# The experts' stage of a hybrid encoder block: pipelined blocks and a scatter that adds

## What is computed

```python
gsel = top-1 of 4 groups                      # per token
eid  = gsel * 8 + top-2 of the 8 experts of that group
gate = p_group * top_p / sum(top_p)
# rows sorted by expert, each expert's rows cut into blocks
y_e  = (silu(xb @ w_gate[e]) * (xb @ w_up[e])) @ w_down[e]
h    = h + sum over the token's two experts of gate * y_e
```

## Time and profile before

| what | value |
|---|---|
| median of 3 runs | 3429.85 us (3428.99 to 3430.35) |
| span of the profiled execution | 3433.8 us |
| PE busy | 3059.8 us, 89% of the span |
| DVE, ACT, POOL busy | 45%, 32%, 10% |
| first gate instruction of `experts` | 2463.71 us |
| last group of down instructions begins | 3424.35 us |

### The profile page before, as it was taken

The page is one execution under the profiler, slowest core; times in us unless marked ns, Lnnn a source line. Parts: engine busy times, 40 slices in busy tenths (PEclk is TensorE's granted clock), DMA queues, the critical chain, the costliest instruction groups (busy, mean ns, idle before and its releaser), DMA issues. The chain is left out here.

```text
span 3433.8 us, 82115 instructions
## 1 busy us (share of the span) xinstructions
PE 3059.8 (89%) x33176; PEld 2305.5 (67%) x33177; DVE 1553.3 (45%) x3540; ACT 1115.5 (32%) x2626; POOL 352.2 (10%) x478
## 2 busy tenths in 40 slices
PE   5999999999968888879999959995399999999999
PEld 4777777777845555578888845553277777777776
DVE  3675666656657777623333337774011111111111
ACT  2343334333447777722222213432011111111111
POOL 0000000000000000000000000000422222222222
PEclk9999999999979999989999989997699999999999
DMA  5211121112130110011111144324577777767663
GB/s 209 65 59 56 52 66 57 57 49 70 57 100 7 48 47 9 9 60 42 42 42 42 41 178 147 135 98 149 75 282 280 283 279 276 283 231 262 218 243 112
DMA packets 211799, 413.98 MB, mean 121 GB/s; under 512 B 29738, under 2 KB 95530, under 8 KB 210016
## 3 DMA queue, kind: packets, MB, share of 16 engines
q1 hardware_dynamic: 191184, 360.07, 30.1%
q0 software_dynamic: 20368, 50.44, 4.2%
HBM read 334.97 MB, written 88.31 MB: 123 GB/s over the span
## 5 line engine op out<-in xcount | busy, mean ns | idle before, releaser
L287 PE MATMUL pj_big<-pj_xnT,pj_w_in 128*128 128x256 f32 x2816 | 646.1, 386 | 10.2 <-issue 8.8
L287 PEld LDWEIGHTS pj_big<-pj_xnT,pj_w_in 128*128 128x128 f32 x2816 | 545.8, 194 | 95.3 <-issue 16.3
L1753 PEld LDWEIGHTS ex_pg<-ex_wg,ex_xT 128*64 128x64 f32 x5120 | 292.1, 137 | 63.9 <-issue 61.2
L1753 PE MATMUL ex_pg<-ex_wg,ex_xT 128*64 128x128 f32 x5120 | 319.7, 275 | 6.8 <-issue 5.4
L1753 PE MATMUL ex_pu<-ex_wu,ex_xT 128*64 128x128 f32 x5120 | 312.9, 273 | 0.0
L1762 PE MATMUL ex_py<-ex_wd,ex_hT 128*64 128x512 f32 x1280 | 310.0, 603 | 1.7
L1753 PEld LDWEIGHTS ex_pu<-ex_wu,ex_xT 128*64 128x64 f32 x5120 | 291.3, 137 | 0.0
L1833 DVE TENSOR_TENSOR ex_hh<-ex_sg,ex_pu 128x128 f32<-128x128 f32 x160 | 46.0, 287 | 484.7 <-PE ex_pu L1753 484.7
L1202 PE MATMUL mg_po<-mg_w_out,mg_mix 128*128 128x512 f32 x512 | 230.2, 609 | 5.6 <-DVE mg_mix L1434 3.9
L708 ACT ACTIVATE at_e<-at_sc,at_nmx 128x512 f32<-128x512 f32 (+3 forms) x320 | 196.4, 620 | 115.2 <-DVE at_nmx L747 115.0
L1805 ACT ACTIVATE ex_sg<-ex_pg 128x128 f32<-128x128 f32 x160 | 44.3, 277 | 581.1 <-PE ex_pg L1753 581.1
(11 more groups left out here) (277 smaller groups left out, 4986.5 us busy)
## 6 DMA issues: line engine op xcount, KB each, us to landing
ex_wg<-in_w_exp_gate SPq DMA_DIRECT2D x32, 2048.0 KB
ex_wu<-in_w_exp_up SPq DMA_DIRECT2D x32, 2048.0 KB
ex_wd<-in_w_exp_down SPq DMA_DIRECT2D x32, 2048.0 KB
chunks_s<-pj_st SPq DMA_DIRECT2D x32, 642.0 KB, 4.0
rw_raw<-chunks_s SPq DMA_DIRECT2D x32, 642.0 KB, 3.9
pj_xt<-in_x SPq DMA_DIRECT2D x20, 512.0 KB, 3.7
qk_s<-pj_qo SPq DMA_DIRECT2D x64, 128.0 KB, 1.9
mg_xin<-in_x SPq DMA_DIRECT2D x8, 1024.0 KB, 6.1
```

The costliest lines, as they stand in the source:

```text
L287: ins = pe.matmul(out, lhs, rhs, start=(k == 0), stop=(k == KC - 1))
L1753: ins = pe.matmul(out[j * BT:(j + 1) * BT, 0:P], lhs, w[:, k, c0:c0 + P], start=(k == 0), stop=(k == KC - 1))
```

## The change

It touches the `experts` stage and, by NB and the rounding of the counts, the table in `dispatch`.

- Gate and up weights lie in one tile `wgu`, and the two products are computed together: one matmul streams 256 columns of gate and 256 of up into one bank `pgu` (`gate_up`, 32 instructions of 512 columns). Silu, the multiplication, the transposes of h and the copy to `hT` are done once for a block, over 256 columns for each partition.
- The blocks overlap on PE: `body(b)` transposes h of block b-1, transposes x of block b+1, computes gate and up of block b, and then the down product of block b-1. The first block's `gate_up` stands ahead of the loops, the last one's `down` behind them. The body that crosses to the next expert (`turn`) uses the new expert's `wgu` and the old one's `wd`. For that, every expert must have two blocks or more, so the count is rounded up to at least 2; NB grows from 96 to 128 and the table with it.
- `acc` is gone. DVE computes `yb` = gate * `py`, and the scatter has `compute_op=ALU.add`: the DMA adds the rows to `out`. x is gathered one block further ahead.
- SP waits for `s_pgu` in place of `s_pu`.

```diff
-NB = 2 * S // BT + NE
+NB = 2 * S // BT + 2 * NE
...
-            chain(dve.tensor_scalar(nb[:, :], nb[:, :], 1.0, None, ALU.add))
+            chain(dve.tensor_scalar(nb[:, :], nb[:, :], 1.0, 1.0, ALU.max, ALU.add))
...
-            for s0, b0, b1 in ((0, 0, 4), (1, 4, NB + 1)):
+            for s0, b0, b1 in ((0, 0, 4), (1, 4, NB + 2)):
...
                 n, first = blocks_of(sp, 4 * i + q - 2)
-                sp.wait_ge(s_pu, 2 * (first + n))
+                sp.wait_ge(s_pgu, first + n)
                 weights_in(sp, bass.ds(EPG * q + i, 1), q % 2)
                 sp.wait_ge(s_py, first + n)
                 weights_out(sp, bass.ds(EPG * q + i, 1), q % 2)
...
-            def rows_acc(x):
-                pool.indirect_dma_start(acc[x][:, :], None, out2, bass.IndirectOffsetOnAxis(idx[:, 0:1], 0),
-                                        bounds_check=LAST, oob_is_err=False).then_inc(s_acc[x], 16)
+            def next_x(b):
+                pool.wait_ge(s_x, 16 * b + 32)
+                pool.sem_inc(s_apart, 1)
+                pool.tensor_copy(idx[:, :], tab[:, bass.ds(b + 2, 1), 0]).then_inc(s_idx, 1)
+                pool.wait_ge(s_idx, b + 3)
+                pool.sem_inc(s_apart, 1)
+                pool.wait_ge(s_px, b + 2)
+                pool.sem_inc(s_apart, 1)
+                gather_x()
...
                 pool.indirect_dma_start(out2, bass.IndirectOffsetOnAxis(idy[:, 0:1], 0), yb[x][:, :], None,
-                                        bounds_check=LAST, oob_is_err=False).then_inc(o_y, 16)
+                                        bounds_check=LAST, oob_is_err=False, compute_op=ALU.add).then_inc(o_y, 16)
...
+            def gate_up(x):
                 for k in range(KC):
                     lhs = xT[:, k % 4, k // 4 * BT:(k // 4 + 1) * BT]
                     for j in range(2):
-                        c0 = 2 * P * j + P * part
-                        ins = pe.matmul(out[j * BT:(j + 1) * BT, 0:P], lhs, w[:, k, c0:c0 + P],
+                        ins = pe.matmul(pgu[j * BT:(j + 1) * BT, :, :], lhs, wgu[x][:, k, :, j * HE:(j + 1) * HE],
                                         start=(k == 0), stop=(k == KC - 1))
...
+            def body(b, x, before, i, y):
+
+                transpose_h(before)
                 pe.wait_ge(s_xT, b + 1)
                 pe.wait_ge(s_x, 16 * b + 32)
                 transpose_x()
+                gate_up(x)
+                down(before, i, y)
...
             pe.wait_ge(s_x, 16)
             transpose_x()
+            pe.wait_ge(s_xT, 1)
+            pe.wait_ge(s_x, 32)
+            transpose_x()
+            pe.wait_ge(s_wi[0], 32)
+            gate_up(0)
...
+            def gate(b, x):
+                dve.wait_ge(s_py, b + 1)
+                dve.wait_ge(o_y, 16 * b + 16)
+                dve.tensor_scalar(yb[x][:, :], py[:, :], tab[:, bass.ds(b, 1), 1], None, ALU.mult).then_inc(s_yb, 1)
...
-                    dve.scalar_tensor_tensor(yb[x][:, :], py[:, :], tab[:, bass.ds(b, 1), 1], acc[x][:, :],
-                                             ALU.mult, ALU.add).then_inc(s_yb, 1)
```

More of the change, by code:

```diff
@@ new lines, in transpose_h, with down @@
+            def transpose_h(b):
+                pe.wait_ge(s_hh, b + 1)
+                pe.wait_ge(s_hT, b + 1)
+                for part in range(2):
+                    ins = pe.transpose(phT[:, part * P:(part + 1) * P], hh[:, part * P:(part + 1) * P], ident[:, :])
+                ins.then_inc(s_phT, 1)
+            def down(b, i, x):
+                pe.wait_ge(s_wo[x], 16 * i + 16)
+                pe.wait_ge(s_yb, b + 1)
+                pe.wait_ge(s_hT, b + 2)
+                for part in range(2):
+                    for j in range(2):
+                        for n in range(2):
+                            ins = pe.matmul(py[n * BT:(n + 1) * BT, :], hT[:, part, j * BT:(j + 1) * BT],
+                                            wd[x][:, 2 * j + part, n * HD:(n + 1) * HD],
+                                            start=(part == 0 and j == 0), stop=(part == 1 and j == 1))
+                ins.then_inc(s_py, 1)
@@ L1784, in body, with rest, turn @@
[L1784 to L1785 removed]
+                gate_up(x)
+                down(before, i, y)
+            def rest(i, x, n, first):
+                with pe.Fori(0, n - 1) as j:
+                    body(below(first + j + 1, NB - 1), x, below(first + j, NB - 1), i, x)
+            def turn(i, x, n, first):
+                pe.wait_ge(s_wi[1 - x], 32 * (i + x) + 32)
+                pe.sem_inc(s_apart_pe, 1)
+                body(below(first + n, NB - 1), 1 - x, below(first + n - 1, NB - 1), i, x)
```

169 lines of the change are left out of this document (71 added, 98 removed).

## The result

The changed kernel takes **3380.94 us** (median of 4 runs, 3375.09 to 3383.68), against 3429.42 us (median of 4) before on the same chip: a ratio of 0.9856, 95% interval 0.9842 to 0.987. Forecast were 3404.2 us with a range of 3388 to 3429.

What follows compares the result with a forecast made beforehand. PE was taken as the bound: blocks falling from 12.02 to 11.53 us save 39.2 over 80, and 13.5 is added, so 3433.8 - 39.2 + 13.5 = 3408.1 of span; the median, 3.95 below, is 3404.2 us, range 3388 to 3429.

Steps and rivals of the forecast that it cites:

- The bound: Experts' stage: PE is busy 49.54 of 50 us and bounds; DVE's addition and the gather of acc are hidden, worth nothing.
- The wide products: Gate and up on PE: 32 wide instructions cost 6.88 us a block, against 7.23 for the narrow ones.
- irregular groups: Gate and up before: groups less regular than clean ones, 0.14 us a block, ascribed to narrow-instruction issue and expected to go.
- rival C: Gate and up: narrow matmuls bound by weight loads, wide ones much cheaper; 320 us go, 3084 us; chance 0.01.
- The stops: PE at the outer loop's turns: 15 of 0.52 us, 0.10 a block, kept unchanged; 0.03 added for loop ends and waits.
- The transposes: PE, each block: six transposes in a row cost 0.156 us each, 0.93 together.
- Table: Start of the stage: the larger table's copy to SBUF, scaled by 126/93, adds 5.9 us.
- Second gather: Start of the stage: PE transposes two blocks before its first product and waits for another gather of x, +3.5 us.
- Filling and the bare copy: Pipeline ends: no down product between the first two gate_up, +1.9 us; copy to hT uncovered at the end, +0.7.
- The last scatter: End of the stage: it adds, with a read of out in front; 2.91 us when plain, +1.5 taken.
- L: Time from an adding scatter's start to its landing, mid-stage; taken as 5 to 7 us, so it costs nothing.
- the threshold of 10.3: Scatter landing time in us up to which the chain of scatters, landing plus 1.2, stays hidden behind PE's block.

Runs made afterwards that it cites:

- after_gather: The changed kernel with the old way of adding: rows of out gathered into acc, added on DVE, plain scatter; 3380.19 us, ratio 0.9856.
- narrow: The changed kernel with its gate and up product split again into four groups of 32 instructions of 128 columns; 3392.91 us, ratio 0.9896.
- before_add: The kernel before with the adding scatter alone, no gather of acc, PE's order and shapes as before; 3424.27 us, ratio 0.9989.
- before_grouped: The kernel before with the second transpose of h moved ahead of all sixteen down instructions; 3390.77 us, ratio 0.987.
- small_table: The changed kernel with NB back at 96, so 93 instead of 126 blocks in the table's long copy; 3380.83 us, one run.
- twice: The changed kernel with each block's rows scattered twice at half the gate, the second after the first has landed; 3637.87 us, ratio 1.0598.
- grouped_add: The kernel before with the second transpose of h ahead of the down product and the adding scatter, no pipelining; 3382.41 us, ratio 0.9858.

## Why the prediction was right and wrong

**The bound: right.** PE bound the stage before and binds it after, and what was hidden (the addition on DVE, the wait for `acc`) gave nothing back as a wait: `after_gather` has the old way of adding and takes the same time.

**The wide products: the price right, the reason wrong.** Expected 6.88, measured 6.92; the narrow ones cost 7.04 in the same order, so the wide form is worth 0.12. The 0.14 a block of irregular groups I put down to an issue that barely keeps up. `narrow` shows no irregular group with the same narrow instructions, and `before_add` has none, with the gather of `acc` gone and the same instructions in the same order. A wrong reason gave nearly the right sum, which is luck: the change also took away, or moved to another place, what went with them. The ratio that the Trainium skill gives in "TensorE: Matmul & The Clock Gate", section "Back-to-back issue gap" (81 and 131 ns at 128 and 512 columns, rival C), does not hold for these float32 products on half arrays: 7.04 against 6.92. The formula for a matmul by itself in the same section of the Trainium skill makes about 56 and 216 ns, and that is what these runs show (0.055 and 0.216 us).

**The stops: the step that failed.** "With the turns of the outer loop left at 0.10 (same number of turns, and the same two reads of block numbers on PE)", and 0.03 more for new waits. I priced a stop by what the loop does and not by how far ahead of the array the sequencer was when it got there. The changed kernel has nearly the same turns (14 for 15) and no stop, since the down product's last wait stands before its first instruction and sixteen instructions, 3.4 us, follow it. Before, that wait ended with 2.24 us of work left. With the 0.03 it is 0.13 a block, 10 us.

**The transposes: the second step that failed.** "Six transposes in a row cost 0.63/4 = 0.156 each". The 0.63 held four transposes (0.44 where another transpose follows, in `before_grouped`), the change to the next shape and some of a short wait; in a longer run the change is paid once. Six take 0.81, not 0.93. With 3.53 for the down product and the change behind it, where I had 3.59, that is 0.18 a block, 14 us. Against these stands 0.04 for the product (6.92 for 6.88). Measured together: the block came out at 11.26 instead of 11.53, 22 of the 26.6 us by which the span was missed.

**What is added.** Table: 5.9 expected; `small_table` shows 1.0, and the other runs up to 1.9. Second gather: 3.5 expected; px to product is now 6.45 instead of 2.43, so 4.0. Not in the sum: PE was at the low clock since before its first transposes, and through the 4.3 us of idle it stayed there. The first product took 9.47 us, 2.4 above the 7.09 of the others, where the kernel before lost 1.7. Filling and the bare copy: 2.6 expected, and seen as 0.94 + 0.25 before the second block's transposes and 0.91 before the last down product, 2.1; this last is the wait for `py`, which the sum did not have, and not the copy. The last scatter: 1.5 expected, 1.8 measured. The first product was forecast near 2473 and came at 2467.98. Of these 5.1 us, 4.3 are the time to the first transposes (1.6 longer than before, not 5.9) and 1.4 the stage's start, which came earlier in this run; 0.5 go the other way, for the second gather.

**The scatter: the number right, by luck.** L was taken at 5 to 7, from the 3.5 of a gather, doubled; the median is 6.1. But the plain scatter of `after_gather` lands after 5.9, and that of the kernel before after 6.0, by the 33 of 80 whose records are whole. So a plain scatter in the middle of the stage takes about 6 us as well, and most of L is not the adding. The Trainium skill, in "Collectives: The Full Stack", section "The bandwidth ceiling: the fold count and why AG ≠ RS ≠ AR", has a reducing transfer at half a copy's rate; scatter against scatter, no run here shows that (medians 6.1 and 5.9, means 6.2 and 5.4). `twice` shows that a chain longer than the block binds; it does not test the threshold of 10.3 itself.

**Chances and range.** The range's low end was made of "no stops at all" and 3 us for a cheap start, but with the transposes at 0.156 and most of the table's 5.9 still charged. Each was a term with one side only: I had put a bound against the gain and none for it.

What each part of the 0.77 us a block is, from the periods: one transpose moved out of the down product 0.53 (12.024 to 11.495, stops among them), no gather of `acc` beside the narrow products, with the scatter that adds in its place, 0.12 (11.495 to 11.376), wide in place of narrow products 0.12 (11.376 to 11.256). The pipelining over blocks has no term of its own (`narrow` has it and `grouped_add` has not, and both are at 11.376); it is what lets the wide form be used.

## What to carry to other kernels

Where an in-order engine is the bound, look at how much work is left when its last wait before a loop's turn ends; a wait in the middle of a product can be free in every view of the waits and still uncover the turn. Put instructions of one shape in one run, and price a run by its length without the change at its end. Before building a pipeline over blocks, try the move of one instruction that gives the same order to the bound engine.

## What the runs showed of the hardware

- An adding indirect scatter of 128 rows of 2 KB is issued by POOL in 1.59 us (plain 1.05) and lands after 2.7 to 8.6 us, median 6.1, with the DMA engines busy for 0.96 of a stretch. A plain one in the same kernel (`after_gather`) lands after 2.2 to 7.7 us, median 5.9, and the period of a block is the same (11.256).
- A turn of the outer loop left PE idle when the last wait ended 2.24 us (15 stops of 0.52) or 1.93 us (14 stops of 0.4) before the next instruction was due, and not at 3.09 or 3.5.
- Float32 matmuls on half arrays cost 0.055 us at 128 columns and 0.216 at 512, from 7.04/128 and 6.92/32: 2% apart per column.
- The time of the table's copy from HBM, with the constants behind it, is not set by the number of its 8-byte pieces alone: 35% more pieces took 5% longer in one pair of runs, 10% in the mean of eleven (21.4 against 19.5 us).
- PE, idle for 81 us, was at the low clock (granted 0.50) before the first transposes of the stage. With a gap of 4.3 us behind these it was granted 0.50 until 2472, 0.80 in the next 2 us and 1.00 from 2474 on; the kernel before, with a gap of 1.3, had 0.66 in 2466 to 2468 and 1.00 from 2468. The first product cost 2.4 us more than a later one, before 1.7.
